# Prompt attention by head pairs in a hybrid decoder step: two row tiles for the scores, two column tiles for the values

## The reference, cut to what matters

```python
s = jnp.einsum('bqhd,bqnhd->bqhn', q, kg).astype(jnp.float32) * (HEAD_DIM ** -0.5)
s = jnp.where(ok[None, :, None, :], s, -jnp.inf)
m = s.max(-1, keepdims=True)
p = jnp.exp(s - m)
den = p.sum(-1, keepdims=True)
o = jnp.einsum('bqhn,bqnhd->bqhd', (p / den).astype(v_src.dtype), vg)
...
wgt = jax.nn.softmax(jnp.stack(lses), axis=0)
o_b = jnp.einsum('gbqh,gbqhd->bqhd', wgt, jnp.stack(outs).astype(jnp.float32))
return jnp.concatenate([o_a, o_b.astype(o_a.dtype)], axis=2)
```

## Time and profile before

| what | us |
|---|---|
| median of 3 runs | 1692.43 (1685.87 to 1697.28) |
| the profiled execution | 1691.04 |
| its span | 1689.3 |
| PE busy, whole span | 1584.1 (94%) |
| DVE / ACT busy, whole span | 927.2 (55%) / 558.7 (33%) |
| prompt attention, from first score product to the first copy of sample keys | 189.0 to 305.8 |

### The profile page before, as it was taken

One profiled execution on the slowest core, in us unless ns is written; L12 is line 12 of the kernel. 1 busy time (PEld: TensorE's weight loads), 2 busy tenths in 40 slices (PEclk: granted clock), 3 DMA queues, 4 the chain that ended last, 5 costly groups with the idle time before them and its releaser, 6 DMA issues.

```text
span 1689.3 us, 24438 instructions
## 1 busy us (share of the span) xinstructions
PE 1584.1 (94%) x9462; PEld 1376.8 (82%) x9462; DVE 927.2 (55%) x1764; ACT 558.7 (33%) x1040; POOL 57.3 (3%) x89
## 2 busy tenths in 40 slices
PE   6999899888899999999979999989989999999995
PEld 5888766656799999987869888856879999998784
DVE  3644243015766666653562286566576666665355
ACT  2222244331333333333222433342133333333321
POOL 0002200000100000000010000000010000000000
PEclk9999899988999999999989899999989999999998
DMA  4223650435222232232221221054122223224211
GB/s 165 97 94 107 233 216 4 137 109 129 70 81 74 77 97 75 74 120 77 78 83 52 66 80 55 26 176 121 50 70 80 74 77 97 75 74 122 75 63 56
DMA packets 150848, 155.80 MB, mean 92 GB/s; under 512 B 7598, under 2 KB 120366, under 8 KB 150542
## 3 DMA queue, kind: packets, MB, share of 16 engines
q1 hardware_dynamic: 146842, 141.70, 27.1%
q0 software_dynamic: 3936, 13.14, 2.4%
HBM read 142.99 MB, written 21.91 MB: 98 GB/s over the span
## 4 chain that ended last, share of the span: by engine, by line
PE 85%; DVE 8%; ACT 4%; issue 2%; DMA 0%; SPq 0%; POOL 0%; DVEq 0%; ACTq 0%; POOLq 0%
PE ps L618 65%; PE ps L599 5%; PE ps L629 4%; PE ps L680 2%; PE ps L787 2%; PE ps L950 1%; DVE x_reg L1570 1%; PE ps L983 1%; PE ps L1014 1%; DVE w_lo L1379 1%; ACT w_hi L1062 1%; DVE x_reg L1574 1%; ACT arena L1095 1%; PE ps L714 1%; DVE arena L1464 1%
## 5 line engine op out<-in xcount | busy, mean ns | idle before, releaser
L618 PE MATMUL ps<-xh_reg,w_hi 128*128 128x288 f32 x1552 | 463.4, 299 | 8.2 <-DVE xl_reg L1386 8.2
L618 PE MATMUL ps<-xl_reg,w_hi 128*128 128x288 f32 x1552 | 458.8, 296 | 0.0
L618 PE MATMUL ps<-xh_reg,w_lo 128*128 128x288 f32 x1552 | 458.8, 296 | 0.0
L618 PE MATMUL ps<-w_hi,xh_reg 128*128 128x512 f32 x768 | 308.7, 402 | 7.9 <-DVE x_reg L1552 3.6
L618 PE MATMUL ps<-w_lo,xh_reg 128*128 128x512 f32 x768 | 302.7, 394 | 0.0
L618 PE MATMUL ps<-w_hi,xl_reg 128*128 128x512 f32 x768 | 302.4, 394 | 0.0
L618 PEld LDWEIGHTS ps<-xh_reg,w_hi 128*128 128x128 f32 x1552 | 293.2, 189 | 10.5 <-DVE xl_reg L1386 5.4
L618 PEld LDWEIGHTS ps<-xl_reg,w_hi 128*128 128x128 f32 x1552 | 293.3, 189 | 0.0
L618 PEld LDWEIGHTS ps<-xh_reg,w_lo 128*128 128x128 f32 x1552 | 292.9, 189 | 0.0
L1379 DVE TENSOR_TENSOR w_lo<-raw,w_hi 128x2048 fp32r<-128x2048 f32 (+1 forms) x52 | 113.7, 2186 | 260.3 <-ACT w_hi L1062 260.3
L618 PEld LDWEIGHTS ps<-w_hi,xh_reg 128*128 128x128 f32 x768 | 146.5, 191 | 40.8 <-issue 8.7
(11 more groups left out here) (176 smaller groups left out, 1649.8 us busy)
## 6 DMA issues: line engine op xcount, KB each, us to landing
raw<-in_ffn_w_up SPq DMA_DIRECT2D x88, 512.0 KB, 5.0
raw<-in_ffn_w_down SPq DMA_DIRECT2D x40, 512.0 KB, 4.6
raw<-in_attn_w_in SPq DMA_DIRECT2D x24, 512.0 KB, 5.0
raw<-in_gla_w_in SPq DMA_DIRECT2D x24, 512.0 KB, 4.4
out_swa_s<-in_state_swa_kv SPq DMA_DIRECT2D x2, 3968.0 KB
x_reg<-in_x_prompt SPq DMA_DIRECT2D x8, 512.0 KB, 5.1
raw<-in_gla_w_out SPq DMA_DIRECT2D x8, 512.0 KB, 4.6
arena<-in_state_swa_kv SPq DMA_DIRECT2D x12, 256.0 KB, 3.3
```

The costliest lines, as they stand in the source:

```text
L618: mm = pe.matmul(out, lhs(i, a), rhs(i, b), start=first and i == 0 and a + b == 0, stop=last and i == ks - 1 and a == 1)
```

## The change

Eight steps take the place of 16: a step n is a query block (n // 2) and a pair of heads (n % 2), and each part is done for both heads b of the pair.

- Scores: the two heads' products of a group follow each other, one on partitions 0 to 63, one on 64 to 127, into two banks. Banks 0 and 1 serve groups 0 and 2, banks 2 and 3 groups 1 and 3, so groups 2 and 3 wait until DVE has read groups 0 and 1, and groups 0 and 1 of the step after next are issued ahead.
- Scores of one pair lie in `s_buf`, of the next in the two halves of `raw`. So SP loads units 12 and 13 after the transposes of the seventh pair, not at once.
- Values: v's 64 columns of one head are the stationary side, the transposed probabilities (`pair_pT[b]`) the moving side; the two heads' outputs go to partitions 0 to 63 and 64 to 127 of one bank (`tile_position` (0, 0) and (0, 64)). The output is feature-major.
- 1/sum lies on the queries' partitions, and is now needed along the free dimension: DVE makes `diag`, the identity times 1/sum, and PE multiplies a matrix of ones with it, again in two column tiles. ACT copies that to `o_scale`, DVE multiplies (`o_pair`), ACT rounds into `xTh`, DVE makes `xTl`. `turn_o`, `o_los` and `o_tok`'s prompt use go.
- POOL writes `ones` once.

```diff
+        pair_scores = [s_buf, raw[:, :, 0:1792]]
...
-            for n in range(2, 14):
+            for n in range(2, 12):
                 load_unit(n)
...
+            sp.wait_ge(turned, PAIR_BATCH[PAIRS - 1])
+            load_unit(12)
+            load_unit(13)
...
+                    if g >= 2:
+                        pe.wait_ge(s_read, 8 * n + 2 * (g - 1))
+                    elif n >= 1:
+                        pe.wait_ge(s_read, 8 * n - 1 + g)
+                    for b in range(2):
+                        rows = slice(HD * b, HD * b + HD)
+                        mm = pe.matmul(ps[:, 2 * (g % 2) + b, 0:(qi + 1) * P - k0], qkT[rows, c, qi * P:(qi + 1) * P],
+                                       qkT[rows, 8 + c, k0:(qi + 1) * P], start=True, stop=True)
+                    mm.then_inc(s_ready, 1)
...
-                        mm = pe.matmul(ps[:, bank, merged * P:merged * P + P], pT[:, i, :],
-                                       v_tok[:, kt, (2 * g + h // 2) * P:(2 * g + h // 2 + 1) * P],
-                                       start=i == mine[0], stop=i == mine[-1])
+                        for b in range(2):
+                            at = (2 * g + pair) * P + HD * b
+                            pe.matmul(ps[HD * b:HD * b + HD, bank, merged * P:merged * P + P], v_tok[:, kt, at:at + HD],
+                                      pair_pT[b][:, i, :], start=i == mine[0], stop=i == mine[-1], tile_position=(0, HD * b))
+                if n == 0:
+                    pe.wait_ge(ones_ready, 1)
+                pe.wait_ge(diag_ready, n + 1)
+                for b in range(2):
+                    mm = pe.matmul(ps[HD * b:HD * b + HD, bank, 256:512], ones, diag[:, b, :], start=True, stop=True,
+                                   tile_position=(0, HD * b))
+                mm.then_inc(scale_done, 1)
...
+            scores(0, range(4))
+            scores(1, range(2))
+            for n in range(PAIRS):
+                turn_probs(n, 0)
+                if n + 1 < PAIRS:
+                    scores(n + 1, range(2, 4))
+                turn_probs(n, 1)
                 values(n)
+                if n + 2 < PAIRS:
+                    scores(n + 2, range(2))
...
+            exps(0, 0)
+            exps(0, 1)
+            for n in range(PAIRS):
+                take_probs(n, 0)
+                if n >= 1:
+                    round_out(n - 1)
+                take_probs(n, 1)
+                if n + 1 < PAIRS:
+                    exps(n + 1, 0)
+                    exps(n + 1, 1)
+                take_scale(n)
+            round_out(PAIRS - 1)
...
+            def scale_diagonals(n):
+                dve.wait_ge(probs, 4 * n + 4)
+                if n >= 1:
+                    dve.wait_ge(scale_done, n)
+                dve.reciprocal(rden[:, 2 * n:2 * n + 2, :], den[:, 2 * n:2 * n + 2, :]).then_inc(vec, vs.one())
+                settle()
+                for b in range(2):
+                    for merged in range(2):
+                        ins = dve.tensor_scalar(diag[:, b, merged * P:merged * P + P], ident[:, :],
+                                                rden[:, 2 * n + b, merged:merged + 1], None, ALU.mult)
+                ins.then_inc(diag_ready, 1)
...
+            first_scores(0)
+            last_scores(0)
+            first_scores(1)
+            for n in range(PAIRS):
+                scale_diagonals(n)
+                if n + 1 < PAIRS:
+                    last_scores(n + 1)
+                if n >= 1:
+                    rest_of_out(n - 1)
+                if n + 2 < PAIRS:
+                    first_scores(n + 2)
+                scale_out_pair(n)
+            rest_of_out(PAIRS - 1)
```

More of the change, by code:

```diff
@@ L388, in build_program @@
         SP_BATCH = -(-len(KEY_BLOCKS) // 4)
-        BATCH_BEFORE_SAMPLE = UP0 + 4 * sum(P_BATCH) + PQ
+        PAIRS = 2 * PQ
+        PAIR_BATCH = [UP0 + sum(2 * P_BATCH[m // 2] for m in range(n)) for n in range(PAIRS + 1)]
+        BATCH_BEFORE_SAMPLE = PAIR_BATCH[PAIRS]
         BATCH_LN0 = BATCH_BEFORE_SAMPLE + 2 * (4 * K_BATCH + SP_BATCH) + 2
@@ L395, in build_program @@
         BATCH_LN2 = BATCH_Y + TURNS_X + 2
-        BATCH_O = [UP0 + 4 * sum(P_BATCH[:qi + 1]) + qi for qi in range(PQ)]
-        LO_BATCHES = ([b for b in range(TURNS_X)] + BATCH_O
+        LO_BATCHES = ([b for b in range(TURNS_X)]
                       + [b0 + b for b0 in (BATCH_LN0, BATCH_LN1, BATCH_Y, BATCH_LN2) for b in range(TURNS_X)])
@@ L663, in _, with pair_buffer, scores @@
                         turn_rope(r)
[L666 to L670, removed]
+            def pair_buffer(n):
+                return pair_scores[(n + 1) % 2]
+            def scores(n, groups):
+                qi, pair = divmod(n, 2)
                 for g in groups:
-                    rows, c = head_rows(g, h)
+                    c = 2 * g + pair
                     k0 = max(0, qi - 1) * P if g == 1 else 0
@@ L689, in prob_blocks, with turn_probs @@
                 return out
+            def turn_probs(n, b):
+                blocks = prob_blocks(n // 2)
+                pe.wait_ge(probs, 2 * (2 * n + b) + 2)
+                for i in range(0, len(blocks), 4):
+                    turn([(j * P, pair_buffer(n)[:, b, col:col + P]) for j, (col, _, _) in enumerate(blocks[i:i + 4])])
             def values(n):
-                qi, h = divmod(n, 4)
+                qi, pair = divmod(n, 2)
                 blocks = prob_blocks(qi)
[L694 to L701, removed]
+                bank = (4, 7)[n % 2]
                 if n >= 2:
-                    pe.wait_ge(o_ready, 2 * (n - 1))
-                bank = (4, 7)[n % 2]
+                    pe.wait_ge(o_made, n - 1)
+                seen = 0
                 for merged in range(2):
-                    mine = [i for i, b in enumerate(blocks) if (b[2] > 0) == bool(merged)]
+                    mine = [i for i, blk in enumerate(blocks) if (blk[2] > 0) == bool(merged)]
                     for i in mine:
@@ L1102, in take_probs @@
+            def take_probs(n, b):
+                nblk = P_BLOCKS[n // 2]
+                if n >= 1 and b == 0:
+                    act.wait_ge(scale_done, n)
                 for b0 in range(0, nblk, 4):
                     k = min(4, nblk - b0)
[L1104 to L1113 removed]
+                    take(pair_pT[b][:, b0:b0 + k, :], lambda bank: bank.rearrange("p (j c) -> p j c", j=4)[:, 0:k, :])
@@ L1486, in o_los @@
-            def o_los(qi):
-                batch_lo(BATCH_O[qi], 0, qi * P, P, [xTl[:, 0:4, qi * P:(qi + 1) * P]])
-            soft_scores(0)
-            for n in range(16):
-                if n % 4 == 0 and n:
-                    o_los(n // 4 - 1)
-                if n + 1 < 16:
-                    soft_scores(n + 1)
-                outputs(n)
-            o_los(PQ - 1)
+                for g in range(2):
+                    for b in range(2):
+                        take_scores(n, g, b)
@@ new lines, in last_scores @@
+            def last_scores(n):
+                for b in range(2):
+                    hn = 2 * n + b
+                    for g in (2, 3):
+                        take_scores(n, g, b)
+                    dve.wait_ge(s_read, 8 * n + 6 + 2 * b)
+                    dve.tensor_reduce(mb[:, hn, 1:2], mx[:, hn, 1:4], AXX, ALU.max).then_inc(vec, vs.one())
+                    settle()
+                    dve.tensor_scalar(nm[:, hn, :], mb[:, hn, :], -ATT_SCALE, None, ALU.mult).then_inc(nm_ready, 1)
@@ L1890, in _ @@
             pool.memset(qz_reg, 0.0).then_inc(qz_zero, 1)
+            pool.memset(ones, 1.0).then_inc(ones_ready, 1)
             new_rows = {0: ("moba", None), 1: ("swa0", 120), 2: ("swa1", 248), 3: ("swa2", 248)}
```

130 lines of the change are left out of this document (62 added, 68 removed).

## The result

| | before | after |
|---|---|---|
| median, us (lowest to highest, 4 runs each) | 1690.54 (1685.87 to 1697.28) | 1648.24 (1645.86 to 1650.8) |
| ratio to before | | 0.9747 [0.9709, 0.9786] |
| profiled execution / its span, us | 1691.04 / 1689.3 | 1647.16 / 1645.3 |
| span ahead of the first score product | 189.0 | 189.7 |
| first score product to the first transposes of probabilities | 3.18 | 4.28 |

42.3 us saved by the medians, 2.5%, where 34.5 were forecast. The stage starts 0.7 us later, and the rest behind it is 2.0 us shorter.

What follows compares the result with a forecast made beforehand. PE's own work was taken as the bound. Eight pairs at 76.2 us against 110.8 save 34.6; start costs 1.1, end gives back 1.0, net 34.5: 1691.0 - 34.5 = 1656.5 us, range 1645 to 1677.

Steps and rivals of the forecast that it cites:

- Value pairs at 0.23: Values on PE: two heads' products in two column tiles take 0.23 us, half of before; bounds 0.23 and 0.46.
- A score pair costs one product: Scores on PE: two heads' products in two row tiles overlap fully; bounds one product or two.
- Start +1.1, end -1.0: Around the eight pairs: first transposes start 1.1 us later; the end, before the sample keys, gives back 1.0 us.
- I give 1.0 us a pair: PE, each pair: gaps for five changes of kind of work and waits on the last copy, 8 us in all.
- the better one: Whole kernel: ACT's and DVE's hand-overs better hidden than the gaps of 1.0 us a pair; 1648 us, chance 0.05.
- The second term: Pairs 0 and 1 (block 0): 8.8 us each, between PE at 1.2 GHz (9.2, 10.4) and some 6.8 at full clock.
- a change of kind on PE: PE order: a change loses a record's tail, 0.06 us; nine fewer would gain 0.5 us a pair, left outside the sum.
- Score pairs that do not overlap: Scores on PE: row tiles run one after the other, 16.7 us more; time 1673, chance 0.15.
- Neither kind overlaps: Scores and values on PE: no tiles overlap, 17 us added to 16.7; time 1690, no change, chance 0.06.
- A new wait: Pairs: the chain through copies and exponentials becomes the bound, about 14 us; time 1671, chance 0.15 shared with longer low clock.
- A low clock through block 1: Pairs 2 and 3: PE's 7.1 and 7.6 us double, 14.7 more; time 1671, chance 0.15 shared with a new wait.
- The low clock throughout: All eight pairs: PE at 1.2 GHz takes 131 us instead of 76.2, 55 more; time 1711, chance 0.04.

Runs made afterwards that it cites:

- e1: Changed kernel with both heads' score products on the lower 64 partitions, so without row tiles: 1666.71 us, +17.9 to the changed kernel.
- e4: Changed kernel plus 21 extra identity products into an unused bank, filling PE's waits around the first scores and pair 0: 1647.71 us.
- e5: Changed kernel with scores of the step after next issued after each sum of the values, instead of behind them all: 1649.65 us.
- e3: Changed kernel with neither row tiles for scores nor column tiles for values (58 of 74 pairs of value products): 1677.51 us, ratio 0.9919 to the kernel before.
- e6: Changed kernel with the rounding of a pair's output moved from ACT to DVE: 1645.86 us.
- e8: Changed kernel with both the extra identity products at the start and the output rounding moved from ACT to DVE: 1643.73 us.

## Why the prediction was right, and where it was off

The direction, the cause and the range held, and the signs in the products appear: the score records of a pair start some 7 ns apart. The periods are shorter than the ones named.

- **PE sets the period, and PE's work shrinks.** Right: PE's busy time in the loop fell from 104.1 to 62.5 us, 41.6 of the 43.0 by which the loop got shorter.
- **Value pairs at 0.23.** Right: 0.22.
- **A score pair costs one product.** Right, and it was the one choice without a row: a group of 512 columns of two heads takes 0.96 us. e1 prices the other end at 11.5 us in pairs 2 to 7, forecast 13.3, and at 17.9 in all, forecast 16.7, with a longer low clock in it.
- **Products of ones, 0.50.** 0.53. **A diagonal, 0.3.** 0.285:

```profile
L1536 DVE TENSOR_SCALAR attn_side<-ident,arena 128x128 f32<-128x128 f32 x32 | 7.0, 285 | 0.3
```

- **DVE and ACT stay behind PE.** Right: of the 53.7 us of pairs 2 to 7 PE is busy 49.7, ACT 40.6, DVE 32.4. The waits in 208 to 261 (who waits for whom: us, times, longest) show DVE and ACT waiting for PE longer than PE for ACT, and a copy of one batch as what PE waits for:

```profile
ACT attn_side L1075 <- PE ps L614: 9.9, 16, 1.7
DVE arena L1500 <- PE ps L701: 5.4, 5, 3.0
PE ps L614 <- ACT attn_side L1075: 3.3, 9, 0.9
```

- **Start +1.1, end -1.0.** 4.28 against 3.18, and 4.16 against 5.0: +1.1 and -0.8. ACT's first copy of sample keys starts at 263.11, where "near 270" had the longer loop in it; before, the first such copy starts at 304.19, which the earlier trace rows leave out.
- **The moved loads cost nothing.** Right: SP issues units 12 and 13 at 249, and the first split of that weight, at 342.87, waits for PE and not for a DMA:

```profile
249.05 2.32 SPq L462 DMA_DIRECT2D raw<-in_attn_w_out  x4
```

```profile
342.87 1.91 ACT L1089 ACTIVATE w_hi<-raw 128x2048 fp32r<-128x2048 f32 x1 [9.17 <-PE ps L790]
```

**Where it was off: the loop at 76.2 us, measured 67.9.** Two terms, by pair (forecast, measured):

| pairs | forecast | measured | difference |
|---|---|---|---|
| 0 and 1 | 17.6 | 14.2 | 3.4 |
| 2 and 3 | 16.7 | 14.7 | 2.0 |
| 4 to 6 | 32.8 | 29.8 | 3.0 |
| 7 | 9.1 | 9.2 | -0.1 |

The failed step is "I give 1.0 us a pair": for pairs 2 to 6 the difference is that microsecond and nothing else. The gaps had been counted already. The transposes were taken at 0.62 us a batch because ACT's copy of 0.60 sets their pace, which holds the waits for the copies; pair 4's two rows of transposes, 1.89 + 1.82 = 3.71, contain the 0.31 and 0.25 us that PE waits, and the sum had 3.7 for them. The other cadences, start to start, held the edges between kinds in the same way. Without the 1.0 the sum for pair 4 is 9.69; measured 9.67. In pair 7 the microsecond was needed: no scores stand between its transposes, and the waits for ACT are longer there (the turns take 5.57 us where the sum had 4.4). The case that the prediction called the better one, 1648, named this error and gave it 0.05. That its time was met as well is luck in part: it took 8 us out of the gaps, where 4.9 of the 8.3 us are gaps and the other 3.4 are the next term.

The second term is the low clock. Pairs 0 and 1 were both taken at 8.8 us, as if the whole of block 0 ran slow. Pair 0 did, 8.52 us at a granted clock of 0.52; then the clock came back at about 202, and pair 1 took 5.64 at 1.00. The 6.8 us that the chain of the other engines was given at full clock were too many as well: in e4 the two pairs take 5.81 and 5.46.

**A step that came out right on a wrong price.** The prediction priced a change of kind on PE at a record's tail, 0.06 us, and set 0.5 us a pair aside for the drain. e5 shows 0.17, so the nine changes fewer would be worth 1.5 us a pair in block 2, or 1.2 for seven: two of the 14 go from values to transposes, both on the whole array, and are no change of tiling. The 1.55 us of records against 1.49 between starts, from which the prediction took its price, already had the edges in both figures. It did not hurt the sum after, since there are only five changes left and the cadences held part of each; as a price of the order of before it was three times too small.

**The rivals.** Score pairs that do not overlap: fell (e1). Neither kind overlaps: fell, and its price of no change was wrong as well, since without any tiles the kernel is still 0.9919 of before (e3). A new wait: fell; e6 took work from ACT and the loop kept its length. A low clock through block 1: fell in both profiled executions, 1.00 from 202 and from 197. The low clock throughout: no run of this kernel is near 1711, but e3's long execution shows that it can hold through a stretch in which PE is busy 15.3 of 16 us, so "against: with such work the clock came back" was too strong an argument.

## What to carry to other kernels

Two products in fp32 that each fill half of the rows or half of the columns of the array cost about the time of one here when they are issued next to each other (1.92 us against 3.63 for four score products; 0.22 for two value products, where one took 0.23), so look for groups in the profile whose shape says 64 on either side, and for what keeps the partner from standing next to them. When a sum is built from start-to-start distances, the waits and edges are in it: add a gap only where the new order opens a wait that the old rows do not have. Order work on TensorE so that products of one kind stand together, and count the changes: they cost 0.17 us each here.

## What the runs showed of the hardware that was not expected

- A change between the kinds of products here (whole array, two row tiles, two column tiles) costs about 0.17 us, with no idle time in the rows that would give it away (e5, and 0.19 for the two edges of a score group on its own side before).
- The time after which the higher clock came back was not a property of the program. Around 191 us PE stood idle and the clock fell in every profiled execution but e4's and e8's; it came back after 14 us before, 10 and 7 in two executions of the changed kernel, 14 in e1, and after some 38 and 14 in two of the kernel without tiles. Only the filled start (e4, e8) kept it through the stage, and in e4 it fell right behind.
